# Sine layers on 128 partitions, the first stages in another order, and the cross attention's projections cut into smaller pieces

## The chip, the cores and the metric

The kernel runs on one core of one Trainium2 chip, in one launch. The metric is the time of an execution in microseconds on the device, from the median of several runs. A core has TensorE (matrix products, called PE in the profile), VectorE (DVE), ScalarE (ACT), GpSimd (POOL) and SyncE (SP, which here issues nearly all transfers). Each engine works through its own instructions in their order and waits on semaphores.

## The reference

Two transformer blocks in a row, float32, on 512 positions of width 1024. What the change touches is the very beginning and the cross attention of the second block:

```python
# first block: filters of the long convolution, from an MLP with sines over the positions
h = jnp.sin(freq * (z @ p["hy_w1"] + p["hy_b1"]))
h = jnp.sin(freq * (h @ p["hy_w2"] + p["hy_b2"]))
h = jnp.sin(freq * (h @ p["hy_w3"] + p["hy_b3"]))
h = h @ p["hy_w4"]
h = h * jnp.exp(-t * deltas)          # then the spectrum of h
...
mod_x = silu_c @ w_mod[l] + b_mod[l]  # shifts, scales and gates, also for ctx
hx = modulate(rmsnorm(x, p["norm_mix"]), sh_a, sc_a)
q_x, k_x, v_x, hy_x = jnp.split(hx @ p["w_in"], cuts, axis=-1)
...
# second block
q = (xn @ w_q).reshape(b, s, XATTN_HEADS, XATTN_HEAD_DIM)
scores = jnp.einsum('bqhd,bkhd->bhqk', q, k) * (XATTN_HEAD_DIM ** -0.5)
p = jax.nn.softmax(scores, axis=-1)
o = jnp.einsum('bhqk,bkhd->bqhd', p, v).reshape(b, s, D_MODEL)
return o @ w_o
```

The MLP is 33 to 64 to 64 to 64 to 2048 wide, over 512 positions. The cross attention has 4 heads of width 256 and 256 memory positions.

## The kernel before, in words

Every engine's program is written out by hand, and so is the order of work. Activations lie transposed: features on partitions, 512 positions along the row. `job_plan` lists all results that TensorE leaves in PSUM, in the order in which they end; a job's number modulo 8 is its bank. `begin(name)` or `open_bank(name)` waits until the job eight places earlier has been taken out of that bank, `end` tells the others that the job is full, `full`, `done` and `evicted` are the waits for it on the other engines. So the list alone decides which earlier result a new one has to wait for.

**The beginning.** SyncE issues the loads in the order written: parameters, positions, `w123` (the first three MLP weights), constants, then slabs of `w_mod` with `w4`, `delta`, x, `dft_k`, ctx between them, then slabs of `w_in`. Slabs of weights are 2 MB and take turns in two slots; a slab's load waits until the slab two before has been used. TensorE does h1, h2, h3 (L943, L947; 64 rows out, 512 positions). Between them VectorE computes the argument of the sine (`sine_argument`: scaling, and taking it back to one turn in seven instructions) and ScalarE the sine. `modulation(s)` multiplies a vector with a slab of `w_mod` (L920: 8 products of 32 columns, spread over four column groups of the array), ScalarE copies the row out, and `modulation_columns(s)` turns it into columns (`modc_s`, L935), to which VectorE adds the bias (`mod_column`). The sixteen jobs `h4_o_t_d` (L955) are the filters for two orders o, four tiles t, two directions d. For each t VectorE multiplies with ScalarE's decays (`decays`), and adds and subtracts the directions: four instructions of 0.69 us. The eight spectra (SPECTRA, L969, jobs `KE..` and `KO..`) are taken out by ScalarE (`spectrum_out`) and VectorE (`spectrum_pair`). `norm_x` and `norm_ctx` are the two RMS norms: ScalarE squares eight tiles, GpSimd adds them up, TensorE sums over partitions with a matrix of ones (L826, L829), ScalarE makes 1/sqrt (`norm_factor`), VectorE multiplies (`normalise`, L2246). Then come k, q, v.

**Split products.** Weights and activations are split into a high part in a rounded format and the remainder as low part; `mm3` does three products (high by high, high by low, low by high; L856 to L858) for one tile k of the width. ScalarE makes the high parts, VectorE the low ones (`split_w` for a slab in two halves, `split_x` for activations).

**The cross attention.** A loop over n = 0 to 17, 16 pairs of head and tile of 128 queries. In step n TensorE computes the scores `xs` of pair n (L1418), transposes the probabilities of pair n - 2 (`xt`, L1390), and after a head's last pair multiplies them with the values (`xo`, L1449: the head product). Between these stand pieces of the query projection of the last four tiles (`xq_4` to `xq_7`, XQ_PARTS) and of the first half of the output projection (`out3a`, XO_FIRST). VectorE and ScalarE do the softmax (`memory_max`, Exp, the scaling at L3017, which reports `p_ready`), ScalarE and VectorE take the transposes and head products out, and split the two slabs of the output weights, at steps 6 and 15. `out3_high` (L1404) and L1456 are the second half of the output projection, which stays open in four banks.

Of the kernel before, what the change touches and what calls it, by code (L numbers as in the profile page):

```python
# [19 lines left out]
P = 128  # L20
# [65 lines left out]
XQ_STEPS = [3, 4, 7, 10]  # L86
XQ_PARTS = {2: (0, 0, 4), 3: (0, 4, 8), 4: (1, 0, 8), 6: (2, 0, 4), 7: (2, 4, 8), 10: (3, 0, 8)}
XO_FIRST = [11, 12, 14, 15]

XO_SPLIT_0, XO_SPLIT_1 = 6, 15  # L90
# [29 lines left out]
def job_plan():  # L120
# [3 lines left out]
    j += ["h1", "h2", "mod_0", "h3", "mod_1"]  # L124
    j += [f"h4_0_{t}_{d}" for t in range(NT) for d in range(2)] + ["modc_0", "mod_2"]
    j += [f"h4_1_{t}_{d}" for t in range(NT) for d in range(2)] + ["modc_1", "mod_3", "modc_2"]
    for n, (o, c, m) in enumerate(SPECTRA):
        j += [f"KE{c}_{o}_{m}", f"KO{c}_{o}_{m}"]
        if n == 1:
            j += ["modc_3", "norm_x"]  # L130
# [198 lines left out]
def two_blocks(nc, io, out_dram):  # L329
# [10 lines left out]
    with ExitStack() as ctx:  # L340
# [21 lines left out]
        ones = sb("ones", [P, P])  # L362
        silu = sb("silu_c", [P, KD, 32])
# [179 lines left out]
        def loaded(eng, name):  # L543
            eng.wait_ge(sem("ld_" + name), 16)
# [46 lines left out]
        norm_acc = {"norm_x": 50, "norm_ctx": 51, "norm_hy": 60, "norm_ffn": 80, "norm_mid": 80, "norm_mix2": 81, "norm_mem": 83, "norm_xa": 83, "norm_mlp": 83, "norm_fin": 83}  # L591
# [40 lines left out]
        def _(sp):  # L632
# [5 lines left out]
            load(w123[0:64, 0:192], io["hy_w123"], "w123")  # L638
            load(con[:], io["consts"], "con")
# [24 lines left out]

            slab("mod", 0, io["w_mod"], 0)
            load(w4[0:64, :], io["hy_w4"], "w4")
            slab("mod", 1, io["w_mod"], 512)
            load(delta, io["delta"].partition_broadcast(P), "delta")
            slab("mod", 2, io["w_mod"], 1024)
            load(xin, io["xT"].rearrange("(k p) t -> p k t", p=P), "x")  # L670
            slab("mod", 3, io["w_mod"], 1536)
            load(Kdft, tables["dft_k"].rearrange("(t p) f -> p t f", p=P), "dft_k")
# [123 lines left out]
        def _(pe):  # L796
# [55 lines left out]

            def mm3(ps, lh, ll, rh, rl, start, stop):
# [84 lines left out]

            pe.wait_ge(sem("ones_ready"), 1)
            loaded(pe, "pos")  # L940
            loaded(pe, "w123")
            ps = begin("h1")
            end(mm(ps[0:64, :], w123[0:33, 0:64], posT[0:33, :].rearrange("p (i e) -> p e i", e=2), start=True, stop=True))  # L943
            for n in (1, 2):
                pe.wait_ge(sem("sin_done"), n)
                ps = begin(f"h{n + 1}")
                end(mm(ps[0:64, :], w123[0:64, 64 * n:64 * n + 64], hT[n - 1][0:64, :], start=True, stop=True))  # L947
                modulation(n - 1)
# [457 lines left out]
            for n in range(XH * NT + 2):  # L1406
# [16 lines left out]
                if n in XQ_PARTS:  # L1423
# [6 lines left out]
                    if n in XQ_STEPS:  # L1430
                        end(ins)
# [1848 lines left out]
```

## Time and profile before

| | |
|---|---|
| runs | 1750.44, 1754.27, 1759.69 us; median 1754.27 |
| profiled execution | 1750.88 us, its span 1749.1 us |
| TensorE busy | 1676.3 us, 96% |
| VectorE, ScalarE, GpSimd busy | 56%, 40%, 8% |
| chain that ended last | TensorE 81%, VectorE 10%, ScalarE 5%, issue 2%, DMA 1% |
| mean granted TensorE clock | 0.981 |

Positions in time are microseconds from the span's start. A float32 product of 512 columns appears as two records of TensorE. Busy shares are means over the span; which wait ends last in a stage has to be read from that stage's rows. The granted clock is 0.50 at 1.2 GHz and 1.00 at 2.4 GHz; ahead of its first change in an execution the profile prints 1.00 whatever it was.

### The profile page before, as it was taken

The page shows a single profiled execution, that of the slowest core. Times are in us where ns is not written, and L with a number is a line of the kernel's source. Part 1 is how long each engine was busy: PE and PEld are TensorE (multiplying, and loading weights), DVE is VectorE, ACT ScalarE, POOL GpSimd, SP SyncE. Part 2 cuts the span into 40 slices and gives each one's busy share as a digit, 9 for nine tenths or more (in the row PEclk, how much of TensorE's full clock was granted, in tenths as well). Part 3 has the DMA queues.
Part 4 walks back from the last instruction along what each step waited for, and adds up shares of the span by engine and source line. Part 5 has one row for each costly group of instructions (what it writes and reads, how often), then busy time and mean ns, then how long its engine had stood idle before and what let it go on. Part 6 is the DMA issues. An engine that isn't in the chain of part 4 may idle for free.

```text
span 1749.1 us, 18829 instructions
## 1 busy us (share of the span) xinstructions
PE 1676.3 (96%) x7214; PEld 1283.1 (73%) x7214; DVE 981.7 (56%) x1350; ACT 693.7 (40%) x1040; POOL 142.7 (8%) x150
## 2 busy tenths in 40 slices
PE   6999998899899999999999999999989999999997
PEld 2477765457688888888788787567866788888885
DVE  5767485576634423445689497566533463636362
ACT  2622354513433313335554667955432331312121
POOL 0312000024300000004000000213000100000001
PEclk7999999899999999999999999999999999999999
DMA  9234212601323233313241121425211232222221
GB/s 340 106 121 145 72 49 74 229 35 48 98 96 96 73 100 117 96 61 108 97 167 48 49 73 42 154 91 192 97 49 49 70 123 96 97 96 96 96 96 48
DMA packets 113240, 174.50 MB, mean 100 GB/s; under 512 B 3787, under 2 KB 56523, under 8 KB 112716
## 3 DMA queue, kind: packets, MB, share of 16 engines
q1 hardware_dynamic: 109404, 160.76, 27.1%
q0 software_dynamic: 3760, 12.72, 2.3%
q8 instruction: 49, 0.80, 0.2%
q14 instruction: 27, 0.22, 0.0%
HBM read 169.00 MB, written 4.46 MB: 99 GB/s over the span
## 4 chain that ended last, share of the span: by engine, by line
PE 81%; DVE 10%; ACT 5%; issue 2%; DMA 1%; POOL 0%; SPq 0%; DVEq 0%; ACTq 0%; POOLq 0%
PE bank L856 16%; PE bank L858 16%; PE bank L857 16%; PE bank L893 6%; PE bank L894 6%; PE bank L898 5%; PE bank L1107 2%; PE bank L1122 1%; PE bank L1049 1%; PE bank L969 1%; DVE weight_slots_lo L2254 1%; PE bank L1061 1%; PE bank L1449 1%; PE bank L1252 1%; PE bank L955 1%
## 5 line engine op out<-in xcount | busy, mean ns | idle before, releaser
L3101 POOL TENSOR_TENSOR arena<-arena 128x512 f32<-128x512 f32 (+1 forms) x56 | 77.4, 1390 | 969.5 <-ACT arena L1550 965.5
L858 PE MATMUL bank<-hx_hi,weight_slots_lo 128*128 128x512 f32 x320 | 125.5, 392 | 0.0
L3056 DVE TENSOR_TENSOR weight_slots_lo<-weight_slots,weights_hi 128x2048 fp32r<-128x2048 f32 x30 | 67.4, 2289 | 98.0 <-ACT weights_hi L2213 98.0
L1519 ACT ACTIVATE weights_hi<-weight_slots 128x2048 fp32r<-128x2048 f32 (+2 forms) x46 | 76.9, 1722 | 111.3 <-DMA weight_slots<-in_ffn_w_down 57.6
L2213 ACT ACTIVATE weights_hi<-weight_slots 128x2048 fp32r<-128x2048 f32 x30 | 55.8, 1908 | 163.5 <-DMA weight_slots<-in_w_up 116.7
L857 PE MATMUL bank<-xn_lo,weights_hi 128*128 128x512 f32 x288 | 112.1, 389 | 0.0
L856 PE MATMUL bank<-sq_hi,weights_hi 128*128 128x512 f32 x256 | 99.6, 389 | 0.0
L857 PE MATMUL bank<-sq_lo,weights_hi 128*128 128x512 f32 x256 | 99.6, 389 | 0.0
L858 PE MATMUL bank<-sq_hi,weight_slots_lo 128*128 128x512 f32 x256 | 99.6, 389 | 0.0
L1505 ACT ACTIVATE arena<-bank 128x512 f32<-128x512 f32 (+2 forms) x110 | 54.7, 539 | 104.0 <-PE bank L858 50.5
L2254 DVE TENSOR_TENSOR weight_slots_lo<-weight_slots,weights_hi 128x2048 fp32r<-128x2048 f32 (+2 forms) x36 | 70.2, 1990 | 26.9 <-ACT weights_hi L1519 26.9
L1550 ACT ACTIVATE arena<-arena 128x512 f32<-128x512 f32 (+1 forms) x80 | 45.8, 584 | 99.2 <-DVE arena L3075 28.2
L893 PE MATMUL bank<-xn_hi,weights_hi 128*128 128x512 f32 x192 | 76.4, 398 | 3.1 <-ACT xn_hi L1535 3.1
L894 PE MATMUL bank<-xn_hi,weight_slots_lo 128*128 128x512 f32 x192 | 76.2, 397 | 0.0
L898 PE MATMUL bank<-xn_lo,weights_hi 128*128 128x512 f32 x320 | 74.2, 389 | 0.0
L2569 DVE TENSOR_TENSOR weight_slots_lo<-weight_slots,weights_hi 128x2048 fp32r<-128x2048 f32 x18 | 40.4, 2288 | 59.7 <-ACT weights_hi L1774 59.7
L3075 DVE TENSOR_TENSOR arena<-bank,arena 128x512 f32<-128x512 f32 x32 | 22.1, 690 | 87.8 <-PE bank L858 87.8
L858 PEld LDWEIGHTS bank<-hx_hi,weight_slots_lo 128*128 128x128 f32 x320 | 60.4, 189 | 13.0
L898 PEld LDWEIGHTS bank<-xn_lo,weights_hi 128*128 128x128 f32 x320 | 60.1, 188 | 12.5
L856 PE MATMUL bank<-hx_hi,weight_slots_lo 128*128 128x512 f32 x160 | 65.3, 408 | 3.7 <-DVE arena L2427 2.7
L856 PE MATMUL bank<-ff_hi,weights_hi 128*128 128x512 f32 x176 | 68.5, 389 | 0.0
L857 PE MATMUL bank<-ff_lo,weights_hi 128*128 128x512 f32 x176 | 68.5, 389 | 0.0
(427 smaller groups left out, 4122.9 us busy)
## 6 DMA issues: line engine op xcount, KB each, us to landing
weight_slots<-in_w_in SPq DMA_DIRECT2D x24, 1024.0 KB, 7.2
weight_slots<-in_ffn_w_up SPq DMA_DIRECT2D x22, 1024.0 KB, 7.1
weight_slots<-in_w_up SPq DMA_DIRECT2D x16, 1024.0 KB, 6.6
weight_slots<-in_w_down SPq DMA_DIRECT2D x16, 1024.0 KB, 6.2
weight_slots<-in_w_mod SPq DMA_DIRECT2D x14, 1024.0 KB, 8.1
arena<-in_w_mod POOLq DMA_DIRECT2D x32, 256.0 KB, 3.2
weight_slots<-in_w_out SPq DMA_DIRECT2D x8, 1024.0 KB, 8.6
weight_slots<-in_w_xkv SPq DMA_DIRECT2D x8, 1024.0 KB, 7.4
```

What stands on the lines that cost most here:

```text
L856: mm(ps, lh, rh, start=start, stop=False)
L857: mm(ps, lh, rl, start=False, stop=False)
L858: return mm(ps, ll, rh, start=False, stop=stop)
L893: mm(ps[:, 0:width], wh(k, m), x2[0][:, k, 0:width], start=k == 0, stop=False)
L894: mm(ps[:, 0:width], wl(k, m), x2[0][:, k, 0:width], start=False, stop=False)
L898: ins = mm(ps[:, 0:width], wh(k, m), x2[1][:, k, 0:width], start=False, stop=k == KD - 1)
L1505: free(A(out, src, ACT.Copy), name)
L1519: A(high_half(kind, n, i), W[:, s_, a:b], ACT.Copy).then_inc(w_hi, 1)
L2213: A(W_hi[:, s % 2, a:b], W[:, s % 2, a:b], ACT.Copy).then_inc(w_hi, 1)
L2254: V.tensor_tensor(low(kind, n)[:, a:b], W[:, s, a:b], high_half(kind, n, i).bitcast(F32), ALU.subtract).then_inc(w_lo, 1)
L3056: V.tensor_tensor(W_lo[:, s % 2, a:b], W[:, s % 2, a:b], W_hi[:, s % 2, a:b].bitcast(F32), ALU.subtract).then_inc(w_lo, 1)
L3101: G.tensor_tensor(acc, acc, sq[i % 2][:, 0:width], ALU.add).then_inc(sq_added, 1)
```

## The change

Three things. The sine layers use all 128 partitions: the even positions on partitions 0 to 63 and the odd ones on 64 to 127, 256 columns each, so that each layer is two products in two quarters of the array; `w123`, `w4` and the biases are loaded twice for it. The first stages are in another order: x is loaded ahead of the `w_mod` slabs, its squares are taken between the sines and summed by TensorE tile by tile (`input_squares`) without GpSimd, and the `modulation` calls stand behind the filters. In the cross attention the pieces of `xq` and `out3a` are smaller and stand in every step from 2 to 15, and the output weights are split by halves at four steps.

```diff
-XQ_STEPS = [3, 4, 7, 10]
-XQ_PARTS = {2: (0, 0, 4), 3: (0, 4, 8), 4: (1, 0, 8), 6: (2, 0, 4), 7: (2, 4, 8), 10: (3, 0, 8)}
-XO_FIRST = [11, 12, 14, 15]
-
-XO_SPLIT_0, XO_SPLIT_1 = 6, 15
+XQ_STEPS = [4, 6, 9, 10]
+XQ_PARTS = {2: [(0, 0, 3)], 3: [(0, 3, 6)], 4: [(0, 6, 8), (1, 0, 1)], 5: [(1, 1, 5)], 6: [(1, 5, 8)],
+            7: [(2, 0, 3)], 8: [(2, 3, 7)], 9: [(2, 7, 8), (3, 0, 4)], 10: [(3, 4, 8)]}
+XO_FIRST = [12, 13, 14, 15]
+XO_PARTS = {11: [(0, 0, 3)], 12: [(0, 3, 4), (1, 0, 2)], 13: [(1, 2, 4), (2, 0, 2)], 14: [(2, 2, 4), (3, 0, 1)], 15: [(3, 1, 4)]}
+
+XO_SPLITS = {7: (0, 0), 9: (0, 1), 13: (1, 0), 15: (1, 1)}
...
-    j += ["h1", "h2", "mod_0", "h3", "mod_1"]
-    j += [f"h4_0_{t}_{d}" for t in range(NT) for d in range(2)] + ["modc_0", "mod_2"]
-    j += [f"h4_1_{t}_{d}" for t in range(NT) for d in range(2)] + ["modc_1", "mod_3", "modc_2"]
+    j += ["h1", "h2", "h3", "norm_x"]
+    j += [f"h4_0_{t}_{d}" for t in range(NT) for d in range(2)] + ["mod_0", "mod_1"]
+    j += [f"h4_1_{t}_{d}" for t in range(2) for d in range(2)] + ["modc_0"]
+    j += [f"h4_1_{t}_{d}" for t in range(2, NT) for d in range(2)] + ["modc_1", "mod_2", "mod_3"]
     for n, (o, c, m) in enumerate(SPECTRA):
         j += [f"KE{c}_{o}_{m}", f"KO{c}_{o}_{m}"]
-        if n == 1:
-            j += ["modc_3", "norm_x"]
+        if n == 0:
+            j += ["modc_2", "modc_3"]
...
             load(w123[0:64, 0:192], io["hy_w123"], "w123")
+            hy_cols = io["params"][0:64, PCOL["hy_b"][0]:PCOL["hy_freq"][1]]
+            for e in range(2):
+                load(hy_par[64 * e:64 * e + 64, :], hy_cols, "hy_par")
+            load(w123[64:128, 0:192], io["hy_w123"], "w123")
             load(con[:], io["consts"], "con")
...
+            load(xin, io["xT"].rearrange("(k p) t -> p k t", p=P), "x")
+            for e in range(2):
+                load(w4[64 * e:64 * e + 64, :], io["hy_w4"], "w4")
+            load(delta, io["delta"].partition_broadcast(P), "delta")
             slab("mod", 0, io["w_mod"], 0)
-            load(w4[0:64, :], io["hy_w4"], "w4")
             slab("mod", 1, io["w_mod"], 512)
-            load(delta, io["delta"].partition_broadcast(P), "delta")
+            load(Kdft, tables["dft_k"].rearrange("(t p) f -> p t f", p=P), "dft_k")
             slab("mod", 2, io["w_mod"], 1024)
-            load(xin, io["xT"].rearrange("(k p) t -> p k t", p=P), "x")
             slab("mod", 3, io["w_mod"], 1536)
...
+            def input_squares(k0, k1):
+
+                ps = open_bank("norm_x") if k1 < KD else begin("norm_x")
+                for k in range(k0, k1):
+                    i = sq_at["norm_x", k]
+                    pe.wait_ge(sq_ready, i + 1)
+                    ins = mm(ps[:], ones[:], sq[i % 2], start=k == 0, stop=k == KD - 1)
+                    if k < KD - 1:
+                        ins.then_inc(sq_used, 1)
+                if k1 == KD:
+                    end(ins)
...
             for n in (1, 2):
                 pe.wait_ge(sem("sin_done"), n)
                 ps = begin(f"h{n + 1}")
-                end(mm(ps[0:64, :], w123[0:64, 64 * n:64 * n + 64], hT[n - 1][0:64, :], start=True, stop=True))
-                modulation(n - 1)
+                for e in range(2):
+                    ins = mm(ps[halves[e], 0:256], w123[halves[e], 64 * n:64 * n + 64], hT[n - 1][halves[e], 0:256],
+                             start=True, stop=True, tile_position=(64 * e, 64 * e))
+                end(ins)
+                if n == 1:
+                    input_squares(0, KD // 2)
+            input_squares(KD // 2, KD)
...
                 act.wait_ge(sem("sin_arg"), n + 1)
-                A(hT[n][0:64, :], sin_u[0:64, :], ACT.Sin).then_inc(sem("sin_done"), 1)
+                A(hT[n][:, 0:256], sin_u[:, 0:256], ACT.Sin).then_inc(sem("sin_done"), 1)
+                if n == 0:
+                    loaded(act, "x")
+                if n < 2:
+                    for k in range(4 * n, 4 * n + 4):
+                        square_tile("norm_x", k, xin[:, k, :], L)
...
-            mod_rows_out(1)
             decays(0)
-            mod_rows_out(2)
+            for s in (0, 1):
+                mod_rows_out(s)
             decays(1)
-            loaded(act, "x")
-            norm_squares("norm_x", lambda k: xin[:, k, :])
-            mod_rows_out(3)
+            for s in (2, 3):
+                mod_rows_out(s)
+            spectrum_out(*SPECTRA[0])
...
-                mod_column(o)
+            for s in range(2):
+                mod_column(s)
...
-                if n in (XO_SPLIT_0, XO_SPLIT_1):
-                    split_w("xo", int(n == XO_SPLIT_1))
+                if n in XO_SPLITS:
+                    slab_, half = XO_SPLITS[n]
+                    split_w("xo", slab_, (half,))
```

TensorE's first rows in the program before (L943 is h1, L947 h2 and h3, L920 `modulation`, L955 the filters h4, L935 `modulation_columns`, L969 the spectra, L826 and L829 the sum of `norm_x`):

```order
1 L943 MATMUL bank<-arena 64x512
2 L947 MATMUL bank<-arena 64x512
3 L920 MATMUL bank<-weight_slots,silu_c 32x512 x8
4 L947 MATMUL bank<-arena 64x512
5 L920 MATMUL bank<-weight_slots,silu_c 32x512 x8
6 L955 MATMUL bank<-arena 128x512 x8
7 L935 MATMUL bank<-pick_rows,arena 128x2 x4
8 L920 MATMUL bank<-weight_slots,silu_c 32x512 x8
9 L955 MATMUL bank<-arena 128x512 x8
13 L969 MATMUL bank<-arena 128x512 x8
```

and in the changed one (L971 and L978 are h1 to h3, L959 `input_squares`, L993 h4, L934 and L949 the modulation, L1008 the spectra):

```order
1 L971 MATMUL bank<-arena 64x256 x2
2 L978 MATMUL bank<-arena 64x256 x2
3 L959 MATMUL bank<-arena,ones 128x512 x4
4 L978 MATMUL bank<-arena 64x256 x2
5 L959 MATMUL bank<-arena,ones 128x512 x4
6 L993 MATMUL bank<-arena 128x512 x8
7 L934 MATMUL bank<-weight_slots,silu_c 32x512 x16
8 L993 MATMUL bank<-arena 128x512 x4
9 L949 MATMUL bank<-pick_rows,arena 128x2 x4
10 L993 MATMUL bank<-arena 128x512 x4
11 L949 MATMUL bank<-pick_rows,arena 128x2 x4
12 L934 MATMUL bank<-weight_slots,silu_c 32x512 x16
```

The eight sums of squares have moved ahead of h4, and all four `modulation` calls behind its first half.

Step 11 of the cross attention on TensorE, with the semaphores it waits for, before (L1418 the scores, L1390 the transposes, then the first rows of `out3a_0`):

```order
3897 L1418 MATMUL bank<-arena 128x256 [waits psum_free5]
3898 L1418 MATMUL bank<-arena 128x256
3899 L1390 MATMUL bank<-consts,arena 128x128 [waits psum_free6,p_ready]
3900 L1390 MATMUL bank<-consts,arena 128x128
3901 L856 MATMUL bank<-ao_hi,weights_hi 128x512 [waits psum_free5,psum_free7,w_lo]
3902 L857 MATMUL bank<-ao_lo,weights_hi 128x512
```

and changed:

```order
3899 L1454 MATMUL bank<-arena 128x256 [waits psum_free5]
3900 L1454 MATMUL bank<-arena 128x256
3901 L1429 MATMUL bank<-consts,arena 128x128 [waits psum_free6,p_ready]
3902 L1429 MATMUL bank<-consts,arena 128x128
3903 L870 MATMUL bank<-ao_hi,weights_hi 128x512 [waits psum_free4,psum_free1,w_lo]
3904 L871 MATMUL bank<-ao_lo,weights_hi 128x512
```

`out3a_0` now ends a step later in the list of jobs, and so lies in another bank: by the two lists the job eight places ahead of it was `xt_1_3` and is now `xo_1_1`.

## Rows read from the trace of the kernel before

**Rows 1.** Page, part 1: busy time of each engine, share of the span, instructions.

```profile
PE 1676.3 (96%) x7214; PEld 1283.1 (73%) x7214; DVE 981.7 (56%) x1350; ACT 693.7 (40%) x1040; POOL 142.7 (8%) x150
```

**Rows 2.** Timeline of TensorE, 0 to 50: start, duration, line, count, idle before.

```profile
4.05 1.94 PE L943 MATMUL bank<-arena 33*64 33x512 f32 x2 [4.05 <-DMA arena<-in_hy_w]
11.51 1.97 PE L947 MATMUL bank<-arena 64*64 64x512 f32 x2 [5.52 <-ACT arena L1584]
13.41 3.63 PE L920 MATMUL bank<-weight_slots,silu_c 128*32 128x512 f32 x16
19.00 1.07 PE L947 MATMUL bank<-arena 64*64 64x512 f32 x2 [1.97 <-ACT arena L1584]
...
25.60 12.54 PE L955 MATMUL bank<-arena 64*128 64x512 f32 x16 [2.20 <-ACT arena L1584]
```

**Rows 3.** Timeline of TensorE, 50 to 125.

```profile
54.61 7.11 PE L969 MATMUL bank<-arena 128*128 128x512 f32 x16
63.62 1.02 PE L935 MATMUL bank<-pick_rows,arena 128*128 128x2 f32 x8 [1.89 <-ACT arena L1505]
64.50 1.90 PE L826 MATMUL bank<-arena,ones 128*128 128x512 f32 x2
...
89.27 0.58 PE L893 MATMUL bank<-hx_hi,weights_hi_k 128*128 128x512 f32 x1
```

**Rows 4.** Timeline of VectorE, 0 to 110: sine argument, filter loop, its end.

```profile
10.38 0.42 DVE L2291 TENSOR_SCALAR arena<-arena 64x512 f32<-64x512 f32 x1
...
28.66 0.69 DVE L2344 TENSOR_TENSOR arena<-bank,arena 128x512 f32<-128x512 f32 x1 [3.78 <-ACT arena L1604]
...
44.96 0.69 DVE L2344 TENSOR_TENSOR arena<-bank,arena 128x512 f32<-128x512 f32 x1 [3.89 <-PE bank L955]
...
56.74 1.64 DVE L2354 TENSOR_TENSOR arena<-arena 128x512 f32<-128x512 f32 x1
58.41 0.17 DVE L2309 TENSOR_TENSOR mod<-bank,params 128x8 f32<-128x8 f32 x1
```

**Rows 5.** Timeline of ScalarE, 0 to 110.

```profile
24.91 0.63 ACT L1584 ACTIVATE arena<-arena 64x512 f32<-64x512 f32 x1 [5.97 <-DVE arena L2291]
...
26.86 1.08 ACT L1505 ACTIVATE arena<-bank 128x512 f32<-128x512 f32 x2
...
74.37 0.42 ACT L1550 ACTIVATE arena<-arena 128x256 f32<-128x256 f32 x1 [0.71 <-POOL arena L3101]
```

**Rows 6.** Windows: busy us of PE, PEld, DVE, ACT, POOL; granted clock; DMA.

```profile
28.00:43.00 15.00, 15.00 (x36) 5.75 (x35) 11.71 (x18) 5.49 (x8) 0.00 (x0) 0.50 1.06 380
...
65.00:66.00 1.00, 1.00 (x2) 0.33 (x1) 1.00 (x3) 0.00 (x0) 0.00 (x0) 0.50 0.00 0
```

**Rows 7.** SyncE's issue of the first `w_mod` slab, and x from issue to landing.

```profile
3.37 0.98 SPq L654 DMA_DIRECT2D weight_slots<-in_w_mod  x2
...
DMA to landing us min/median/max: 14.6/14.6/14.6
```

**Rows 8.** TensorE's waits, 1240 to 1420 (total us, times, longest); two head products.

```profile
PE bank L1449 <- ACT arena L1505: 5.2, 4, 1.6
PE bank L1390 <- DVE arena L3017: 3.1, 2, 2.8
PE bank L1404 <- DVE arena L2965: 1.0, 1, 1.0
...
1294.18 3.67 PE L1449 MATMUL bank<-arena 128*128 128x512 f32 x8 [1.56 <-ACT arena L1505]
...
1312.13 6.27 PE L1449 MATMUL bank<-arena 128*128 128x512 f32 x8 [1.33 <-ACT arena L1505]
```

**Rows 9.** Timelines, cross attention: VectorE's slab split, scores of step 11, low parts.

```profile
1304.77 4.48 DVE L2254 TENSOR_TENSOR weight_slots_lo<-weight_slots,weights_hi 128x2048 fp32r<-128x2048 f32 x2
...
1324.80 1.02 PE L1418 MATMUL bank<-arena 128*128 128x256 f32 x4
...
1326.85 1.28 DVE L2997 TENSOR_TENSOR ao_lo<-bank,ao_hi 128x512 fp32r<-128x512 f32 x2
```

## What the change will do, told before it was run

> **What bounds the kernel now.** I read the page first: TensorE is busy 96% of the span [rows 1]. So nothing can be won but the few stretches in which it waits or runs at half its clock. Its rows in order of time, beginning and middle, show where these are: ahead of the k product at 89.27 [rows 3], and in the cross attention around 1280 to 1360 [rows 8]. The change touches just these two places; behind each of them both orders are the same, so what is won there moves the rest forward whole. The reader is to take from the rows what ends each wait.
>
> The beginning is a chain, not a throughput. TensorE does three small products at 4.05, 11.51 and 19.00, and waits for the sines in between (idle 5.52 and 1.97 us; `mod_0` and `mod_1` fill the rest) [rows 2]. VectorE then takes the filter products out from 28.66 to 58.41, waiting 3.89 us for `h4_1` in the middle because `mod_2` stands ahead of it on TensorE [rows 4]. The spectra run 54.61 on, are broken by a wait of 1.89 us and by the two sums of `norm_x`, and hand over to k at 89.27 [rows 3]. The granted clock is 0.50 all through 28 to 43, and again behind the wait at 62, in 65 to 66 [rows 6]. Two levels, then: 1.2 GHz (0.5) and 2.4 GHz (1.0).
>
> **The change part by part: the start.**
> 1. h1 waits for `w123` twice, and three small loads more stand ahead of the second. Two issues take 0.98 us [rows 7], so I add 1.6 with the gaps between them: h1 moves from 4.05 to 5.65.
> 2. A sine layer is now 7.46 us from product to product (4.05 to 11.51). VectorE has 4.8 of it (from the product's end at 5.99 to 10.80 [rows 2, 4]). Its instructions lose half their columns and gain half the partitions. The cost per instruction lies between one half (2.4) and unchanged (4.8); ScalarE's rows give 0.42 for 256 columns against 0.63 for 512 [rows 5], two thirds, and I take that, as the nearest: 3.1. The product goes from 1.94 to about 1.0 at 1.2 GHz and from 1.07 to 0.55 at 2.4 GHz [rows 2], since the two halves use different columns of the array (if they run one behind the other, 1.94 and 1.07 stay). Sin goes from 0.63 to 0.42. A layer is 4.7 us: h2 at 10.35, and h3 could start at 15.05.
> 3. It doesn't, since ScalarE has a wait for x and four squares between the first Sin and the second, and TensorE four sums of them ahead of h3. x is the first big load now. `mod_0`, which had that place, was there by 13.41 with its issue at 3.4; x is issued 1.5 us later: 14.5. The ends are 13 and 19.5 (issue at 4.9 plus the 14.6 us that x took behind a full queue [rows 7]). A sum over one tile takes 1.9 us at 1.2 GHz [rows 3, 6], 0.2 of it beside the next: 1.7, so 0.87 at 2.4. Two squares fit ahead, so the sums pace: 14.5 + 0.6 + two at 1.7 + two at 0.87 = 20.2. I take the higher clock for the second pair because it was granted to h3 at 19.00 (1.07 us against 1.94) after the 3.63 us of `mod_0` [rows 2]. h3 ends at 20.8, its argument is ready at 23.9, the other four sums end at 24.3, Sin at 24.4, h4 starts at 24.5 (now 25.60).
> 4. Between the end of Sin (25.54) and the loop's start (28.66 [rows 4]) lie 3.1 us now, a table load, two row copies of 1.08 [rows 5] and the first decay; the copies go behind the decays, so it is 2.1: VectorE's filter loop starts at 26.6.
> 5. The loop itself takes 29.75 us less the 3.89 wait, less 0.2 at the second product and 1.0 by which one instruction is drawn out (1.64 instead of 0.69 [rows 4]) while GpSimd adds the squares of `norm_x`, which it no longer does: 24.5. The wait goes only if `h4_1` is there by 26.6 + 12.3 = 38.9. At 2.4 GHz h4_0 takes 7.1 (half of the half clock's 12.54 is 6.3 [rows 2]; the spectra's rate, 16 records in 7.11 [rows 3], is the safer row), to 31.6; `mod_0` and `mod_1`, half of 3.63 each, to 35.3. So yes. The loop ends at 51.1 instead of 58.41.
> 6. What is late next: the spectra's first bank is the one of `modc_0`, and VectorE frees it only behind both loops. TensorE has done `mod_3` by about 47 and waits: spectra at 51.4, against 54.61, 3.2 us earlier.
> 7. From there to k it is 34.66 us now. It loses the two sums (3.4) and the wait (1.9), gets `modc_2` (1.0, the row at 63.62 [rows 3]) and, after 4 us of idling, most likely a stretch at 1.2 GHz as at 65, price 1.7 (half of the 3.4 that the sums took in it): 32.1. k at 83.5: **5.8 us earlier**. ScalarE's side stays close behind: ctx squares at 1.13 us per tile (0.71 wait and 0.42 [rows 5]), eight of them behind the k split, end near 82; 1 to 2 us more if they slip.
>
> **The cross attention.** TensorE waits 5.2 us for copies ahead of the head products, 3.1 for probabilities (2.8 of it once) and 1.0 ahead of `out3_high` [rows 8]. Behind the 2.8 the head product takes 6.27 us instead of 3.67 [rows 8], a trough of the clock: 2.6. Together 11.9. The 2.8 comes from both halves of a slab split in one step, 4.48 us on VectorE [rows 9], at steps that have no filler. Now every step has 9 to 15 products (2.1 to 3.5 us) between the transposes and the next, more than the copy's 1.6, and each half of the split costs 2.24 with a filler over it. The 5.2 and the 3.1 go, but 0.3. In their place come three waits. `xq_5` is opened within step 4, in the bank of `xt_0_2`, 0.35 us too early. `out3a_0` is opened in step 11 in the bank of `xo_1_1`, where it had the bank of a transpose before; VectorE frees that with the low parts of head 1, which now end 3.33 us behind the start of that step's scores (1324.80 to 1328.13 [rows 9]), while TensorE has 1.0 us of work: 2.3. And at step 16 the 1.0 becomes 2.0, since a half split stands in VectorE's queue at step 13, ahead of the residuals. Sum 4.9 or so; 11.9 less 4.9 is **7.0 us** (3 to 9.5: the lower end if the 2.3 us wait brings a trough again and the splits push two steps, the upper if neither).
>
> The sum is 1750.9 - 5.8 - 7.0 = 1738.1 for an execution like the profiled one, whose own time is the low end of the runs; the median stands 3.4 above it. I put the forecast between, at 1740.
>
> A rule against the row: the Trainium skill (TensorE: Matmul & The Clock Gate, Part 1) has a busy engine raised to its full clock and an idle one lowered. The row of 28 to 43 differs: 15.00 us busy of 15.00, and 0.50 all along, while the h4_0 products ran. By the page h4_0 gets the full clock soon after it starts, and the sum stays 1738; by the row it has it only if the clock has risen before it.
>
> **The rivals.**
> - *The low clock stays through h4_0* (15%). For it: the row of 28 to 43. Against it: some five us of sums now stand ahead, and the clock was up (1.07 us for h3) after the 3.63 us of `mod_0` [rows 2]. h4_0 then takes 12.5 us, to 37.1, `mod_0` and `mod_1` 3.6 and 1.8, `h4_1` is there at 43.5, VectorE waits 4.7: the start gives 1.1, the time is 1745.
> - *x is late* (10%). Each us behind 14.5 is one on the path; at 19.5 the start gives 0.8: 1745. Nothing else of the start can help then, as Sin stands behind x in ScalarE's queue.
> - *The cross attention only moves its waits* (8%): the 2.3 us wait and two split steps bring the trough back, 3 us are left: 1744.
> - *Both do better* (9%): x at 13, no trough, the bank wait short: 9 + 9.5, 1733.
> - *Slower* (4%): the clock stays at 1.2 GHz beyond h4_0, into the spectra. Their 64 records at 0.44 us are 28 us; at the low clock they are 56. It turns the sign when more than 26 us of TensorE's work ahead of k are at 1.2 GHz that the forecast has at 2.4 (half of it is the 13 us won). With all the spectra: 1750.9 + 28 + 4 - 7 = 1776. Against it: the first 16 of their records took 7.11 us, at the full clock, right behind small products of `modulation` [rows 3].
> - The change does nothing: no chance of its own, as the waits it moves are in the rows.
>
> **How the numbers follow.** The forecast has 54%. Its own range is 1735 to 1745. The three cases with a smaller gain, at 1744 and 1745, have 33% together, the better one 9%, the slower one 4%. The outer ends come from the bounds: 13 to 18 us won at best, 1731, and at worst 0.8 plus 3 with the median's 3.4 on top, 1750. I give 1730 to 1750. 0.5% is 8.8 us, about what a measurement of this kernel can tell from no change. The forecast (54%), the better case (9%) and a third of the three small-gain cases (11%) are beyond it: 0.74. Same: 0.22. Slower: 0.04.
>
> **What would show each step.** h1 near 5.7; h2 near 10.4; the first L959 sum near 15, h3 near 20, h4 near 24.5; granted clock 1.0 from about 18; VectorE's first L2390 at 26.6 and no wait in the loop; spectra (L1008) at 51.4 with a wait ahead of some 4 us on VectorE; k (L907) at 83.5. In the cross attention: no wait at the L1488 products, one of 2.3 ahead of the first `out3a` product, the stage 7 us shorter. Wrong would be: squares with a table load of their own, h3 behind 22, a wait at `h4_1`, or a stretch behind k that grows by what the start gave.

## The result and the profile after

The changed kernel takes 1740.2 us (median of 4 runs, 1738.75 to 1741.94), the kernel before 1755.1 (median of the 4 runs beside it, 1750.44 to 1759.69): a ratio of 0.992, 95% interval 0.991 to 0.994. The forecast was 1740, the range 1730 to 1750. The profiled execution of the changed kernel took 1738.75 us, with a span of 1736.9; that of before had 1749.1. The span is 12.2 us shorter: k starts 5.9 us earlier (83.38 against 89.27), the cross attention takes 7.0 us less (89.1 to 82.1, from its first scores to the third `out3_4` product), and what lies between and behind takes 0.7 us more. In the series below, with 7 to 16 runs of before each, its median is 1752.6 to 1753.5 us, so the gain is rather 13 us than the 14.9 of these two medians.

TensorE's timeline after, 0 to 50 and 50 to 86; L971, L978, L993, L934, L949, L1008 and L907 answer to L943, L947, L955, L920, L935, L969 and L893 of [rows 2, 3], L959 are the sums over the squares of x:

```profile
5.78 1.12 PE L971 MATMUL bank<-arena 33*64 33x256 f32 x4 [5.78 <-DMA arena<-in_hy_w]
10.67 1.12 PE L978 MATMUL bank<-arena 64*64 64x256 f32 x4 [3.77 <-ACT arena L1627]
16.08 6.03 PE L959 MATMUL bank<-arena,ones 128*128 128x512 f32 x8 [4.29 <-ACT arena L1593]
22.04 0.65 PE L978 MATMUL bank<-arena 64*64 64x256 f32 x4
22.62 3.83 PE L959 MATMUL bank<-arena,ones 128*128 128x512 f32 x8
26.48 5.52 PE L993 MATMUL bank<-arena 64*128 64x512 f32 x16
...
40.12 6.07 PE L993 MATMUL bank<-arena 64*128 64x512 f32 x8
...
53.38 3.67 PE L1008 MATMUL bank<-arena 128*128 128x512 f32 x8
...
83.38 0.58 PE L907 MATMUL bank<-hx_hi,weights_hi_k 128*128 128x512 f32 x1
```

The reader is to see what has no bracket. Behind 16.08 TensorE does not wait again before k. VectorE's rows (the wait of 3.89 us for `h4_1` is gone [rows 4]), then ScalarE's with x:

```profile
28.56 0.69 DVE L2390 TENSOR_TENSOR arena<-bank,arena 128x512 f32<-128x512 f32 x1 [2.59 <-PE bank L993]
...
53.07 0.24 DVE L2355 TENSOR_TENSOR mod<-bank,params 128x8 f32<-128x8 f32 x2
```

```profile
15.40 1.15 ACT L1593 ACTIVATE arena<-arena 128x512 f32<-128x512 f32 x2 [4.78 <-DMA arena<-in_xT]
```

The loop starts where it did (28.66 before) and ends 5.3 us earlier. It ends at 53.07 and TensorE has done `mod_3` at 53.3: two limits at one place. The windows, with the granted clock third from the end:

```profile
28.00:41.00 13.00, 13.00 (x64) 5.50 (x63) 11.73 (x18) 8.80 (x14) 0.00 (x0) 1.00 0.93 335
42.00:51.00 9.00, 9.00 (x29) 3.61 (x32) 8.43 (x14) 3.88 (x6) 0.00 (x0) 0.50 1.04 355
```

At 28 to 41 the clock is 2.4 GHz where before it was 1.2 GHz [rows 6]; it falls at 41, and TensorE had been busy without a gap for 25 us. TensorE's waits of the cross attention, 1230 to 1400, answering to [rows 8]:

```profile
PE bank L870 <- issue: 2.2, 1, 2.2
PE bank L1443 <- DVE arena L3013: 0.9, 1, 0.9
PE bank L1429 <- DVE ao_lo L3045: 0.8, 1, 0.8
PE bank L870 <- DVE weight_slots_lo L3105: 0.4, 1, 0.4
PE bank L1429 <- DVE arena L3065: 0.3, 1, 0.3
```

The 0.4 for the weights' low part comes at 1397.57, 45 us behind the end of the stage, and is not counted in it. Behind the 2.2 the next products are drawn out, at the low clock:

```profile
1314.31 0.63 PE L870 MATMUL bank<-ao_hi,weights_hi 128*128 128x512 f32 x1 [2.19 <-issue]
1314.74 0.63 PE L871 MATMUL bank<-ao_lo,weights_hi 128*128 128x512 f32 x1
...
1319.35 0.40 PE L871 MATMUL bank<-ao_lo,weights_hi 128*128 128x512 f32 x1
```

**An account that holds for all kernels below.** Ahead of k, three numbers: TensorE's waits (from the view of waits, 0 to k); the clock's loss (1 minus the granted clock, summed over windows of one us, which is what the same work would have saved at 2.4 GHz); and the rest, TensorE's own work. The records print 1.00 up to some 20 us although most products there take the time of 1.2 GHz, so that part lies in the rest.

| | k at | waits | clock's loss | rest |
|---|---|---|---|---|
| before | 89.3 | 15.6 | 12.0 | 61.7 |
| changed | 83.4 | 13.8 | 5.1 | 64.4 |
| start_only | 83.9 | 13.1 | 6.8 | 64.0 |
| cross_only | 92.1 | 16.1 | 15.4 | 60.6 |
| bank | 84.2 | 18.3 | 1.7 | 64.2 |
| bank2 | 83.0 | 13.5 | 5.1 | 64.4 |
| whole | 83.7 | 13.6 | 5.1 | 65.0 |
| old_fill | 84.7 | 13.8 | 6.8 | 64.1 |
| sines64 | 94.7 | 13.5 | 13.6 | 67.5 |
| ahead | 88.5 | 14.7 | 6.8 | 67.0 |
| ahead_gp | 86.3 | 24.4 | 1.7 | 60.2 |
| pairs | 83.1 | 18.1 | 3.4 | 61.6 |
| best_start | 82.1 | 18.4 | 1.7 | 62.0 |
| both | 82.3 | 18.5 | 1.7 | 62.1 |

The rest is the same within 1.1 us for kernels with the same beginning (60.6 and 61.7; 64.0 to 65.0), so the account carries. The 5.9 us of the beginning are 1.8 of waits plus 6.8 of clock less 2.7 of more work (among it eight sums on TensorE, where there were two). The same account of the cross attention: 9.4 of waits, 3.4 of clock and 76.2 of work before; 4.2, 1.7 and 76.2 after.

### The profile page after: what moved, and what is told of

Its sections match the earlier page's. It is cut to its first block, busy times and chain, and to the rows that moved or that the text cites. A ratio compares the mean times of both kernels' runs of the same rounds, so it can differ in the third digit from the quotient of the medians.

```text
span 1736.9 us, 18861 instructions
## 1 busy us (share of the span) xinstructions
PE 1670.0 (96%) x7232; PEld 1283.7 (74%) x7232; DVE 973.5 (56%) x1350; ACT 693.6 (40%) x1040; POOL 135.3 (8%) x144
## 4 chain that ended last, share of the span: by engine, by line
PE 83%; DVE 8%; ACT 5%; issue 2%; DMA 2%; SPq 0%; DVEq 0%; ACTq 0%
PE bank L870 16%; PE bank L872 16%; PE bank L871 16%; PE bank L907 6%; PE bank L908 6%; PE bank L912 5%; PE bank L1146 2%; PE bank L1008 2%; PE bank L1161 1%; PE bank L1088 1%; PE bank L1100 1%; DVE weight_slots_lo L2300 1%; PE bank L1291 1%; PE bank L993 1%; PE bank L1488 1%
## 5 line engine op out<-in xcount | busy, mean ns | idle before, releaser
L3150 POOL TENSOR_TENSOR arena<-arena 128x512 f32<-128x512 f32 (+1 forms) x50 | 70.2, 1412 | 971.3 <-ACT arena L1593 968.0
L907 PE MATMUL bank<-xn_hi,weights_hi 128*128 128x512 f32 x192 | 75.8, 395 | 3.1 <-ACT xn_hi L1578 3.1
L912 PEld LDWEIGHTS bank<-xn_lo,weights_hi 128*128 128x128 f32 x320 | 60.1, 188 | 12.5
```

The source lines that it names most:

```text
L907: mm(ps[:, 0:width], wh(k, m), x2[0][:, k, 0:width], start=k == 0, stop=False)
L912: ins = mm(ps[:, 0:width], wh(k, m), x2[1][:, k, 0:width], start=False, stop=k == KD - 1)
L3150: G.tensor_tensor(acc, acc, sq[i % 2][:, 0:width], ALU.add).then_inc(sq_added, 1)
```

## The experiments

**The two parts apart.** start_only is the changed kernel with the old tables and functions of the cross attention; cross_only is the reverse:

```diff
-XQ_PARTS = {2: [(0, 0, 3)], 3: [(0, 3, 6)], ...
-XO_SPLITS = {7: (0, 0), 9: (0, 1), 13: (1, 0), 15: (1, 1)}
+XQ_PARTS = {2: (0, 0, 4), 3: (0, 4, 8), 4: (1, 0, 8), ...
+XO_SPLIT_0, XO_SPLIT_1 = 6, 15
```

> The new beginning with the cross attention of before. If the two parts add up, the first k product (L907's counterpart) stays at 83.4 us, the cross attention takes 89.1 us from its first scores to the third out3_4 product as before, and the span is 1749.1 - 5.2 = 1743.9 us (5.9 won ahead of k, 0.6 given back before the cross attention); the time lies 0.3% under before. If they interact (the beginning shifts phases that the later stages depend on), the stage differs from 89.1 by more than 1 us.

> The beginning of before with the new cross attention. If the two parts add up: k at 89.3 us, cross attention 82.1 us instead of 89.1, span 1742.1 us, time 0.4% under before. If not, the stage is off 82.1 by more than 1 us, or the 2.2 us wait ahead of the first out3a_0 product is gone.

Measured: start_only 1747.1 us (ratio to before 0.996, 0.995 to 0.998), cross_only 1745.9 (0.995, 0.994 to 0.997). The two ratios multiply to 0.991, the changed kernel's is 0.992: the parts add up. The stages say so more closely: k at 83.9 and the cross attention 88.8 us in start_only, 82.2 in cross_only. The spans came out 4.4 and 3.3 us over what was expected. In cross_only that was the beginning of before, 2.8 us later than in its own profile, all of it the clock (15.4 against 12.0). In start_only it was the stretch from k to the cross attention, code that the change doesn't touch: 1190.4 us against 1185.6 before and 1186.2 after, with 17.0 us of clock's loss in it against 13.7 and 10.3. Over all kernels here this stretch took 1184.9 to 1190.5 us. So one profile's span can't tell parts of 2 us. The stage of the cross attention can: it took 82.1 to 82.2 us in six profiles of the changed tables, and 83.8 in a seventh (ahead), which had 1.7 us more of low clock. The beginning is between the two: six executions of the same program up to k have it at 83.0 to 84.7.

**The bank of `out3a_0`.** In the changed kernel it is opened in step 11 in the bank of `xo_1_1`; here it ends in that step and so has the bank of `xq_6`:

```diff
-XO_FIRST = [12, 13, 14, 15]
-XO_PARTS = {11: [(0, 0, 3)], 12: [(0, 3, 4), (1, 0, 2)], 13: [(1, 2, 4), (2, 0, 2)], ...
+XO_FIRST = [11, 12, 13, 15]
+XO_PARTS = {11: [(0, 0, 4)], 12: [(1, 0, 4)], 13: [(2, 0, 4)], 14: [(3, 0, 2)], 15: [(3, 2, 4)]}
```

> The changed kernel with out3a_0 whole in step 11 (its bank is then that of xq_6, long free, not that of xo_1_1), out3a_1 in 12, out3a_2 in 13, out3a_3 in halves in 14 and 15. Theory: the 2.2 us wait is one for the bank, and the 8 head products behind it (3.46 us instead of 1.9) pay for a low clock that the wait brings. Then both go, 3 to 3.8 us less than the changed kernel, less some 0.2 us where steps 14 and 15 have only 1.4 us of filler: span near 1733.7. Rival: the wait is one for the low parts of head 1 as an operand, not for the bank; then it comes back ahead of the third inner tile of the same product, nearly as long, and the time stays within 1 us.

TensorE's timeline of bank, the beginnings with a wait, 1300 to 1350:

```profile
1315.17 0.51 PE L870 MATMUL bank<-ao_hi,weights_hi 128*128 128x512 f32 x1 [0.16 <-DVE ao_lo L3045]
1333.78 0.44 PE L1429 MATMUL bank<-consts,arena 128*128 128x128 f32 x2 [0.87 <-DVE arena L3065]
1335.77 0.47 PE L1443 MATMUL bank<-ao_hi,weights_hi 128*128 128x512 f32 x1 [1.55 <-DVE arena L3013]
```

The wait was for the bank: the operand alone costs 0.16. But the stage is only 1.2 us shorter (80.9), since the two waits of step 16 grew from 1.7 to 2.4 and the low clock came there instead (1336.5 to 1339.9, again 1.7 us). The time, 1739.0 us, can't be told from 1740.2. The expected 3.2 us failed mostly on the clock, which I had tied to the one wait. TensorE's timeline ahead of the spectra, needed further below:

```profile
52.53 5.37 PE L1008 MATMUL bank<-arena 128*128 128x512 f32 x8 [3.94 <-DVE mod L2355]
```

**bank2: the first half of slab 1 is split at step 12.**

```diff
-XO_SPLITS = {7: (0, 0), 9: (0, 1), 13: (1, 0), 15: (1, 1)}
+XO_SPLITS = {7: (0, 0), 9: (0, 1), 12: (1, 0), 15: (1, 1)}
```

> Kernel bank with the first half of slab 1 split at step 12 instead of 13. There VectorE waited 5.6 us for the scores ahead of step 13's maximum, while the split at 13 put the probabilities of step 14 and the residuals behind it 0.87 and 1.55 us late for TensorE. Theory: the split goes into that idle time and the two waits fall to 1 us together or less: stage 79 to 80 us instead of 80.9. Rival: the waits at steps 15 and 16 come from the copies and low parts alone; then the stage stays at 80.9 or a wait turns up at step 13.

TensorE's waits:

```profile
PE bank L1443 <- DVE arena L3013: 1.3, 1, 1.3
PE bank L1429 <- DVE arena L3065: 0.3, 1, 0.3
```

The stage takes 78.0 us, its waits are 1.8 together (1.3 ahead of `out3_high`), and there is no low clock in it at all; kernel both, with the same tables, repeats this. Of bank's two waits one is gone and the other 0.2 shorter, so they fell to 1.3, not to 1.0 as the theory had it. The same split of 2.29 us a step later cost 1.1 us of waits and a trough of 1.7. The time, 1737.0 us, alone would not tell the two kernels apart.

**whole: both halves in one step, the filler as changed.**

```diff
-XO_SPLITS = {7: (0, 0), 9: (0, 1), 13: (1, 0), 15: (1, 1)}
+XO_SPLITS = {7: (0, (0, 1)), 13: (1, (0, 1))}
```

> The changed kernel with both halves of slab 0 split at step 7 and both halves of slab 1 at step 13, 4.5 us of VectorE in one piece, the filler unchanged. Theory: filler of 2.1 to 3.5 us a step covers a half split (2.3) and not a whole one; TensorE waits 1 to 2 us for probabilities after each, and one of the waits brings the clock down: 3 to 6 us more than the changed kernel. Rival: with filler in every step the queue of VectorE catches up and nothing changes (under 1 us); then the halves were not needed.

One execution. The stage takes 87.1 us, 5.0 more. The split at step 7 costs nothing, the one at 13 does; TensorE's waits and VectorE's split:

```profile
PE bank L1429 <- DVE ao_lo L3045: 3.0, 1, 3.0
```

```profile
1331.90 4.49 DVE L2300 TENSOR_TENSOR weight_slots_lo<-weight_slots,weights_hi 128x2048 fp32r<-128x2048 f32 x2
```

That is 2.2 us more of waits and 3.4 more of low clock (5.1 against 1.7, 1339 to 1346 behind the 3.0); the work came out 0.6 less.

**old_fill: the half splits with the steps of before.**

```diff
-XQ_STEPS = [4, 6, 9, 10]
-XO_FIRST = [12, 13, 14, 15]
+XQ_STEPS = [3, 4, 7, 10]
+XO_FIRST = [11, 12, 14, 15]
```

> The changed kernel with xq_4 to xq_7 and out3a_0 to out3a_3 put back into the steps of before (nothing in steps 5, 8, 9, 13), the half splits and the order of the head products kept. Theory: the filler removed the waits for probabilities and for copies, so TensorE waits again at transposes and head products in the steps without filler, 4 us or more in all, and the stage takes 86 us or more instead of 82.1. Rival: the half splits did most of it; then the stage stays within 2 us of 82.1.

One execution. The stage takes 84.6 us: 2.5 more than changed, 4.5 less than before, between the two expectations. The copies' wait is back at three head products, the one for the split is gone:

```profile
1291.34 3.67 PE L1487 MATMUL bank<-arena 128*128 128x512 f32 x8 [1.56 <-ACT arena L1547]
1308.53 3.67 PE L1487 MATMUL bank<-arena 128*128 128x512 f32 x8 [3.36 <-ACT arena L1547]
```

So the filler takes away 6.5 us of waits for copies, the half splits the 2.8 for probabilities and the 3.4 of clock's loss that followed it, though 2.0 of the 2.8 turn up again ahead of the next head product (3.36, where before had 1.33). The changed kernel gets less than the sum, as its filler brought the wait of 2.2 and a trough.

**sines64: the sine layers on 64 partitions again.**

```diff
-                A(hT[n][:, 0:256], sin_u[:, 0:256], ACT.Sin).then_inc(sem("sin_done"), 1)
+                A(hT[n][0:64, :], sin_u[0:64, :], ACT.Sin).then_inc(sem("sin_done"), 1)
```

> The changed kernel with its three sine layers on 64 partitions and 512 columns again; loads, sums and order as changed. Theory: the squares of x stand between the first and the second Sin, so only the first and the third layer count. x is there at 15.4 anyway, and the first Sin (near 13) is still ahead of it, so the first sum stays near 16; behind h3 the longer sine puts h4 at 22.5 + 4.8 + 0.6 or so, 28 instead of 26.5, and TensorE waits some 1.5 us there. k comes 1 to 2.5 us later than 83.4. Rival: the sine layers are what the beginning won; then k is 5 us later or more.

k at 94.7 and 1754.1 us in one execution, 11.3 us later, where I expected 1 to 2.5. By the account 8.5 of them are clock, 3.0 are TensorE's work, and the waits are 0.3 less. The wait behind h3 was 1.8, as expected. The work: the small products take 2.1 us longer, and `h4_0` no longer gets the 1.9 us that experiment pairs explains; that is 4.0 together, and where 1.0 of it was made up is not shown. Windows of sines64:

```profile
30.00:43.00 13.00, 13.00 (x28) 4.12 (x30) 11.45 (x17) 5.73 (x9) 0.00 (x0) 0.50 0.40 145
43.00:50.00 7.00, 7.00 (x37) 3.03 (x30) 3.07 (x5) 3.85 (x6) 0.00 (x0) 0.97 0.78 271
51.00:63.00 12.00, 12.00 (x39) 4.62 (x41) 8.26 (x15) 3.42 (x5) 0.00 (x0) 0.50 0.88 303
```

Twice the low clock for 13.7 us, while TensorE was busy: the first time from 29.79, 2.0 us behind the wait of 1.8, the second time from 50.27 without a wait ahead. With one execution I can't say how much of this belongs to the kernel and how much to that execution.

It also shows what the low clock does to `h4_0` in the new order, TensorE and VectorE:

```profile
27.82 12.11 PE L986 MATMUL bank<-arena 64*128 64x512 f32 x16 [1.76 <-ACT arena L1620]
46.66 0.69 DVE L2383 TENSOR_TENSOR arena<-bank,arena 128x512 f32<-128x512 f32 x1 [4.50 <-ACT arena L1646]
```

VectorE's wait in the middle of the loop is back, 4.50 us. The decay that ended it stood in ScalarE's queue behind the row copy of `mod_1`, which TensorE had ready only at 45.2.

**ahead: the second and third Sin no longer behind x.**

```diff
-                if n == 0:
+                if n == 1:
                     loaded(act, "x")
-                if n < 2:
-                    for k in range(4 * n, 4 * n + 4):
+                    for k in range(3):
                         square_tile("norm_x", k, xin[:, k, :], L)
...
+                    if 2 <= i < 7:
+                        square_tile("norm_x", i + 1, xin[:, i + 1, :], L)
```

> The changed kernel with the second and third Sin no longer behind x: three squares of x between the second and the third Sin, the other five among the first decays; the eight sums on TensorE partly behind h3, partly between the first h4_0 products. The same work in another order. h3 then starts near 15.5 and VectorE's filter loop near 22.5 instead of 27.7 to 28.6. Theory: TensorE is without a wait from its first sum to k, so its own work sets k; only the gap ahead of h3 is won or lost, and k stays between 81.5 and 84.5. Rival: VectorE's loop sets k; then k is 5 us earlier, 78.5.

The loop starts at 22.63 and k at 88.5: both theories fell. 1746.0 us, 5.8 more than the changed kernel. The loop, now early, waits 6.5 us in itself (3.7 for h4 products behind sums, 2.8 for a decay that stands in ScalarE's queue behind the row copy of `mod_1`), TensorE's rest is 2.5 us larger, the clock's loss 1.7 and the waits 0.8. Of the 2.5, 2.1 are `h4_0`: in three pieces it takes 7.7 us instead of 5.5, for the reason that experiment pairs shows.

**ahead_gp: the same, the squares added up by GpSimd.**

```diff
+            add_squares("norm_x")
             add_squares("norm_ctx", CTX)
```

> As ahead, with the squares of x added up by GpSimd as before the change, so that TensorE has two sums of norm_x instead of eight (some 5 to 7 us less work at the beginning), behind the h4_0 products. Theory: with TensorE's work out of the way the loop's start counts: loop from near 22.5, drawn out by 1 to 2 us by GpSimd's adds, to near 48.5; k near 79, time 4 us under the changed kernel. Rival: the adds slow VectorE by more than they save and the low clock lasts longer, k at 83 or later.

k at 86.3, 1744.2 us. The work is down to 60.2 and the clock's loss to 1.7, but the waits are 24.4, and VectorE's loop now is the limit: it runs 24.40 to 55.96, 31.6 us against 24.5, with three instructions drawn out by GpSimd's adds, 3.6 us of wait for the same decay and the rest for h4. VectorE's timeline of ahead_gp:

```profile
27.53 1.18 DVE L2399 TENSOR_TENSOR arena<-arena 128x512 f32<-128x512 f32 x1
28.75 1.64 DVE L2400 TENSOR_TENSOR arena<-arena 128x512 f32<-128x512 f32 x1
...
43.71 0.69 DVE L2390 TENSOR_TENSOR arena<-bank,arena 128x512 f32<-128x512 f32 x1 [3.61 <-ACT arena L1653]
```

**pairs: the h4 products two by two on the two halves.**

```diff
+H4_ROWS = (0, 2, 1, 3)
+H4_JOBS = [(t, d) for two in (H4_ROWS[:2], H4_ROWS[2:]) for d in range(2) for t in two]
```

> The changed kernel with the h4 products in another order, all else alike: the rows 0, 2, 1, 3 instead of 0, 1, 2, 3, and two by two one product on partitions 0 to 63 and one on 64 to 127 (t0, t2, t0, t2, t1, t3, t1, t3). The changed kernel's h4_0 took 5.45 us for 16 records where four of one half took 1.9; if products of the two halves run side by side when they stand next to each other, 8 of them take 3.6 to 4 us at the full clock instead of 5.45, and the first four of h4_1 1 us instead of 1.9. Rival: they don't (the 5.45 has another cause); then 8 take 5.4 or 7.2. On the time: VectorE's loop ends near 52.5 as before, so TensorE only waits longer ahead of the spectra, and k stays within 1.2 us of 83.4 in either case.

TensorE's timeline of pairs, and of both (below) at the full clock, where 8 records are four products:

```profile
26.23 4.34 PE L995 MATMUL bank<-arena 64*128 64x512 f32 x16
...
53.13 3.24 PE L1010 MATMUL bank<-arena 128*128 128x512 f32 x7 [3.00 <-DVE mod L2357]
```

```profile
39.56 1.99 PE L996 MATMUL bank<-arena 64*128 64x512 f32 x8
```

Four products take 2.0 us in this order and 3.70 in the changed kernel's. They do run side by side, and the changed kernel has one such place, where its h4_0 products change from partitions 0 to 63 to 64 to 127: the fifth starts at 28.30 together with the third, the sixth with the fourth, and the eight take 5.45 us instead of the 7.4 of twice 3.70. The Trainium skill (TensorE: Matmul & The Clock Gate, Part 3) says that small products in distinct row groups of the array overlap; the trace agrees, 1.99 against 3.70. The time stays (k at 83.1, 1739.2, one execution): TensorE's rest fell by 2.8 us and it waits 3.0 us ahead of the spectra for VectorE's loop, and 1.8 for a bank in h4_1.

**best_start: both limits moved.** ahead and pairs together, the late squares spread further, and the two row copies moved behind the ninth decay:

```diff
+                    if i == 10:
+                        norm_factor("norm_x")
+                    if i in (10, 12):
+                        mod_rows_out(i // 2 - 5)
```

> The changed kernel with both limits of its beginning moved: the sines ahead of the squares of x as in ahead, the five late squares one by one among the first decays with their sums between the h4_0 products, the row copies of mod_0 and mod_1 and the factor of norm_x behind the ninth and eleventh decay, and the h4 products two by two on the two halves. Theory: the changed beginning has two limits within 1 us of each other, VectorE's loop (to 52.2 to 53.1) and TensorE's work (to 53.3 with some 10 us of it at 1.2 GHz). With both moved the loop runs 22.6 to 47.5 without a wait over 0.5 us, the spectra start at 48 to 50, k at 78.5 to 80.5, and the time is 3 to 5 us under the changed kernel. Rival: the clock takes back what the order gives (a longer low stretch, as in ahead, where 14 us at 1.2 GHz stood against 10); then k stays at 83 or later.

The loop runs 23.12 to 49.6, with a wait of 1.8 us in it, and k is at 82.1, the time 1736.2 us (0.991 of before, 0.988 to 0.994). I expected k at 78.5 to 80.5. It lies 0.9 us below the earliest of the six executions of the changed beginning (83.0), and kernel both repeats it (82.3); the interval of the time alone overlaps the changed kernel's. How much the row copies and the spread squares did was not tried apart. Neither theory named what came next, the slab of `mod_3`:

```profile
48.59 3.27 PE L938 MATMUL bank<-weight_slots,silu_c 128*32 128x512 f32 x16 [4.02 <-DMA weight_slots<-in_w_mod]
```

**both: best_start, bank2, and the loads of ctx and rope behind the first k slab.**

```diff
+            slab("k", 0, io["w_in"], 512)
             load(ctxT, io["ctxT"].rearrange("(k p) t -> p k t", p=P), "ctx")
             load(tiles(82, 2), io["rope"].rearrange("(a p) t -> p a t", p=P), "rope")
-            slab("k", 0, io["w_in"], 512)
```

> The beginning of best_start, the cross attention of bank2, and one move more: the loads of ctx and of the rope tables are issued behind the first k slab instead of ahead of it. In best_start TensorE waited 4.0 us for the w_mod slab of mod_3, which shared the DMA queues with these 1.5 MB (they moved at 325 to 396 GB/s from 36 to 56 us); without them it should land 2 to 4 us earlier, TensorE's wait shrinks to 0 to 2 us, and the spectra start at VectorE's loop end, near 50.1, instead of 51.8: k near 80.3. The cross attention is a stage of 78 to 79 us instead of 82.1. The sum against the changed kernel's profiled span of 1736.9: 3 + 3.5 = 6.5 us less, span 1728 to 1732, time 1.2% under before and 0.5% under the changed kernel. Rival: what the beginning wins is given back ahead of the cross attention, or k is held by the squares of ctx, which now come later; then the span is 1733 or more.

1732.5 us (5 runs, 1732.3 to 1736.9), a ratio to before of 0.989 (0.988 to 0.991), and the lowest median here, 7.7 us under the changed kernel's (5.4 by the two ratios, as the runs are of different series). The cross attention takes 78.0 us without low clock. The span of 1730.5 was forecast (1728 to 1732), k not (82.3 against 80.3): 1.2 us of the 6.4 between the two spans lie in the stretch from k to the cross attention, which no edit touched. The move of the loads did nothing: TensorE waits 4.07 us for the slab as it did 4.02. What was issued behind it had not slowed it. It is the second of two slabs, together 4 MB, issued at 34.2 when `mod_0` and `mod_1` set their slots free. At the 383 to 414 GB/s moved from 37 to 46 these alone take some 10.6 us (an estimate from that rate) of the 12.7 from 36 to 48.7; what the other 2 are stays open:

```profile
34.22 2.64 SPq L666 DMA_DIRECT2D weight_slots<-in_w_mod  x4
```

## Why the prediction was right

The time was right, and most waits went for the reasons given. But in each half of the sum two errors cancelled: in the beginning 2.0 us against 2.1, in the cross attention 0.9 against 1.0.

- **h1 and the sine layer** (steps 1, 2): h1 at 5.78 (5.65 said), h2 at 10.67 (10.35), the argument 3.23 us (3.1), the halves of a small product side by side (1.12 us, not 1.94). Right.
- **x and the sums** (step 3): x at 15.40 (14.5), and nearly three of the four first sums at 1.2 GHz, where I had two (6.03 us, 5.1 said; the records there start 0.85 us apart up to 20.5 and 0.43 from 21.1). h3 at 22.04 was just beyond the 22 that I had named as a sign of being wrong. h4 at 26.48 where I had 24.5: the term was mis-sized by 2.0 us.
- **The loop's start** (step 4): 28.56, not 26.6, as it hangs on step 3. Nothing was won there against 28.66.
- **The loop** (step 5): 24.5 us, to the tenth, without a wait (the terms as I gave them add up to 24.7). This was the enabling gain.
- **What is late next** (steps 6, 7): I had TensorE idle for 4 us ahead of the spectra, at 51.4, and a trough of 1.7 behind it. In the profile it did not wait, since 5.1 us had gone to the low clock at 41 to 51, and there was no trough: 30.0 us from spectra to k, 32.1 said. The 2.1 gave back the 2.0 of step 3. Kernel bank, whose beginning is the same program, took the course I had described: no low clock at 36 to 50, a wait of 3.94 us, the spectra at 52.53, a trough of 1.7 at 53 to 56, k at 84.2. Both courses end within 0.9 us of each other. In the one TensorE's work is the limit, in the other VectorE's loop; the prediction knew only the second.
- **The cross attention**: 7.0 us said, 7.0 measured. Waits of 4.2 (4.9 said) took the place of 9.4; the 2.2 for the bank of `xo_1_1` (2.3 said) and 1.7 at step 16 (2.0) stood where they were put, and bank showed the first to be the bank; the 0.35 for the bank of `xt_0_2` did not come. Not in the forecast sum was the 1.7 us trough behind the 2.2, which I had only as the lower end. So the new side cost 5.9 where I had 4.9, and the old side 12.8 (9.4 and 3.4) where I had 11.9, as its trough cost 3.4 and not the 2.6 I had charged. The 7.0 held by luck of size, not of mechanism.
- **Clock**: the rival that the low clock stays through h4_0 did not come; nor did the one that ends slower. But the clock turned out to be the larger part of the gain at the beginning (6.8 us, against 1.8 of waits), where the prediction spoke of VectorE's wait. The wait is gone because h4_0 ran at 2.4 GHz (5.5 us, not 12.5). The order alone doesn't do it: two slabs' products stand ahead of h4_1 now (3.64 us), and sines64, with the same order and h4_0 at 12.1 us, has a wait of 4.50 there, close to the 4.7 of the rival (one execution).

What stays open: why the clock falls while TensorE is busy without a gap. Six executions of one and the same beginning (changed, start_only, bank, bank2, whole, old_fill) lost 1.7, 5.1 or 6.8 us to it. Kernels with another beginning lost 1.7 to 15.4. The Trainium skill (TensorE: Matmul & The Clock Gate, Part 1) has an idle engine lowered; most troughs behind waits agree (behind 3.94 us in bank, 4.02 in best_start, 2.98 in whole), though pairs had none behind its 3.00; these long stretches of 10 to 14 us don't.

## What to carry to other kernels

Where an engine is busy 96% of the time, account for each stage in waits, low clock and work before crediting an edit: here six sums more were paid for by the clock, and ahead, ahead_gp and pairs, which went at one of the two limits each, won nothing, while best_start, which went at both, won some 1 us at k. Put a long side job into a step where its engine is seen to wait for the engine that bounds (the same 2.3 us cost 1.1 of waits and a trough of 1.7 more at step 13 than at step 12), and see whose bank an early opened product gets. If a contraction has only 64 rows, order the products so that neighbours use different halves.

## What the runs showed of the hardware

- Two f32 products of 64 rows on different halves of the array run side by side if they are neighbours in the queue: four in 1.99 us against 3.70. So did products two places apart: in the changed kernel the fifth started with the third, at 28.30. Both halves of h2 write one bank, at different partitions, and still overlap (1.12 us for both, 1.97 before).
- The granted clock fell from 2.4 to 1.2 GHz with TensorE busy without a wait for 25 us (at 41 in the changed kernel), stayed for 10.2 us, and rose again under the same load. Five of six executions of this beginning had such a stretch, of 10.2 or 13.7 us, at a cost of 5.1 or 6.8 us; bank's had none.
- GpSimd's adds draw out VectorE's instructions on SBUF: in ahead_gp those of two inputs from 0.69 to 1.18, 1.64 and 1.69 us, and two of one input (128x256, at 17.48 and 18.38) from 0.29 to 0.87 and 1.38. One that read a bank meanwhile (26.16) kept its 0.69.
- Loads issued later did not delay a slab: with 1.5 MB issued from 38.6 on (best_start) or from 45.7 on (both), the slabs issued at 34.1 and 34.2 let TensorE go on at 48.59 and 48.74.
